# Inverting triangles as 64x64 diagonal blocks in a two-layer hybrid decoder kernel on one core

## What is computed

```python
def step(S, inp):
    r_t, w_t, k_t, v_t, kk_t, a_t = inp
    sa = jnp.einsum('bhvk,bhk->bhv', S, -kk_t)
    S = S * w_t[:, :, None, :] + sa[..., None] * (kk_t * a_t)[:, :, None, :] + v_t[..., None] * k_t[:, :, None, :]
    return S, jnp.einsum('bhvk,bhk->bhv', S, r_t)
```

## Time and profile before

| what | value |
|---|---|
| median of 3 runs | 1758.09 us (1756.2 to 1758.63) |
| the profiled execution's own time | 1759.65 us |
| its span, first to last instruction | 1757.8 us |
| TensorE busy | 97% |
| VectorE (DVE) busy | 74% |
| ScalarE (ACT) busy | 58% |
| chain that ended last | PE 86%, DVE 6%, ACT 4%, issue 2%, DMA 1% |
| granted TensorE clock, mean | 0.988 of full speed |

### The profile page before, as it was taken

The page is one execution under the profiler, slowest core; times in us unless marked ns, Lnnn a source line. Parts: engine busy times, 40 slices in busy tenths (PEclk is TensorE's granted clock), DMA queues, the critical chain, the costliest instruction groups (busy, mean ns, idle before and its releaser), DMA issues.

```text
span 1757.8 us, 27919 instructions
## 1 busy us (share of the span) xinstructions
PE 1700.0 (97%) x10846; PEld 1516.8 (86%) x10846; DVE 1294.9 (74%) x1185; ACT 1027.5 (58%) x995; POOL 0.9 (0%) x8
## 2 busy tenths in 40 slices
PE   7999999999999899999999999999999999999997
PEld 7999888889999899988888888888888888888885
DVE  5856665475445675757646889888898989898987
ACT  5563454454344456445444677767777777777775
POOL 0000000000000000000000000000000000000000
PEclk9999999999999999999999999999999999999999
DMA  8433331456565443333145889999998999999993
GB/s 287 144 98 108 109 120 61 166 164 196 175 191 185 136 159 116 101 120 121 49 145 197 322 329 392 343 362 375 337 393 319 375 332 392 335 364 355 363 387 137
DMA packets 252072, 411.25 MB, mean 234 GB/s; under 512 B 8400, under 2 KB 133712, under 8 KB 251344
## 3 DMA queue, kind: packets, MB, share of 16 engines
q1 hardware_dynamic: 249728, 401.20, 64.8%
q10 hardware_dynamic: 2256, 8.82, 1.3%
HBM read 407.89 MB, written 2.10 MB: 233 GB/s over the span
## 4 chain that ended last, share of the span: by engine, by line
PE 86%; DVE 6%; ACT 4%; issue 2%; DMA 1%; SPq 0%; DVEq 0%; ACTq 0%
PE W L459 18%; PE W L461 18%; PE W L460 18%; PE Y L459 6%; PE Y L460 6%; PE Y L461 6%; PE Y L681 2%; PE Y L675 2%; PE W L568 1%; ACT w_hi L1116 1%; PE Y L568 1%; PE Y L650 1%; DMA raw<-w_in 1%; DVE xt L1744 1%; PE Y L912 1%
## 5 line engine op out<-in xcount | busy, mean ns | idle before, releaser
L1585 DVE TENSOR_TENSOR w_lo<-raw,w_hi 128x2048 fp32r<-128x2048 f32 x114 | 261.2, 2292 | 197.4 <-ACT w_hi L1116 196.3
L459 PE MATMUL W<-w_lo,x_hi 128*128 128x512 f32 (+1 forms) x1120 | 390.3, 349 | 1.3 <-DVE x_lo L1883 1.1
L461 PE MATMUL W<-w_hi,x_hi 128*128 128x512 f32 (+1 forms) x1120 | 386.0, 345 | 0.0
L460 PE MATMUL W<-w_hi,x_lo 128*128 128x512 f32 (+1 forms) x1120 | 385.6, 344 | 0.0
L1592 DVE TENSOR_TENSOR w_lo<-raw,w_hi 128x2048 fp32r<-128x2048 f32 x144 | 329.7, 2289 | 45.1 <-ACT w_hi L1122 45.0
L1122 ACT ACTIVATE w_hi<-raw 128x2048 fp32r<-128x2048 f32 x144 | 276.1, 1917 | 73.1 <-PE Y L461 40.0
L459 PE MATMUL W<-x_lo,w_hi 128*128 128x256 f32 x992 | 292.9, 295 | 10.2 <-DVE w_lo L2104 8.9
L1592 DVE TENSOR_TENSOR w_lo<-raw_more,w_hi 128x2048 fp32r<-128x2048 f32 x120 | 275.0, 2292 | 28.5 <-ACT w_hi L1122 28.3
L460 PE MATMUL W<-x_hi,w_lo 128*128 128x256 f32 x992 | 282.8, 285 | 0.0
L461 PE MATMUL W<-x_hi,w_hi 128*128 128x256 f32 x992 | 282.5, 285 | 0.0
L1122 ACT ACTIVATE w_hi<-raw_more 128x2048 fp32r<-128x2048 f32 x120 | 230.5, 1921 | 64.0 <-PE W L461 41.1
(11 more groups left out here) (306 smaller groups left out, 2025.0 us busy)
## 6 DMA issues: line engine op xcount, KB each, us to landing
raw<-w_in SPq DMA_DIRECT2D x124, 512.0 KB, 4.6
raw<-moe_gate SPq DMA_DIRECT2D x48, 1024.0 KB, 6.1
raw<-moe_up SPq DMA_DIRECT2D x48, 1024.0 KB, 6.7
raw<-moe_down SPq DMA_DIRECT2D x48, 1024.0 KB, 5.0
raw_more<-moe_gate SPq DMA_DIRECT2D x40, 1024.0 KB, 7.2
raw_more<-moe_up SPq DMA_DIRECT2D x40, 1024.0 KB, 6.7
raw_more<-moe_down SPq DMA_DIRECT2D x40, 1024.0 KB, 6.0
raw<-w_branch SPq DMA_DIRECT2D x24, 512.0 KB, 4.6
```

The source lines that it names most:

```text
L459: nc.tensor.matmul(out_ap, lhs[0], rhs[1], start=start, stop=False)
L460: nc.tensor.matmul(out_ap, lhs[1], rhs[0], start=False, stop=False)
L461: return nc.tensor.matmul(out_ap, lhs[0], rhs[0], start=False, stop=stop)
L1585: V.tensor_tensor(w_lo[u % 3][:], raw[u % 3][:], w_hi[u % 3][:].bitcast(F32), ALU.subtract)\
```

## The change

- **Form.** The inverse of a 128x128 triangle is put together from its two diagonal blocks of 64x64. `ac` holds those blocks of A, for each u the upper one in partitions 0 to 63 and the lower one in 64 to 127; `compact` (ScalarE, two copies per pass) fills it. `xt`, `xn` (X), `mc` (masked A, and later the product) have 64 columns per u.
- **Levels 1 to 5** work on both blocks: per u two products of 64x64 by 64x64 (`blocks`), one on rows 0 to 63 into partitions 0 to 63, one on rows 64 to 127 into 64 to 127 of the same bank. Copies, additions and masks have half the columns.
- **The turned form** is no longer a transposition but such a product with the identity, in two halves.
- **Level 6** (`TOP`) computes the off-diagonal block: per u one product of 64x64 from the full `sc` with output in partitions 64 to 127, a copy of 64 rows by ScalarE, one product back into partitions 0 to 63, and a copy by DVE into a second column block of `xt`. ScalarE copies the lower diagonal block beside it.
- **`cu`** has two products per head: 64 rows and 64 weight columns for the first half of the output, 128 rows and 64 weight columns for the second.
- **Order.** `compact` stands after the second `scores` entry of each pass; in pass 0 conv 2 is split into front and back, and `masks` stands between them. On DVE the split of weights in the front of conv 2 therefore comes ahead of the masks.
- **Memory and constants.** `dsh` and `td` move under `pr`; `fin1` and `fin2` lie in `mc` and `xn`. The masks are loaded in compact form: the constants come in 6 transfers in place of 1.

```diff
...
-C_COS = C_LEV + LEVELS * P
+C_COS = C_LEV
+D_COS = C_LEV + LEVELS * P
+TOP = LEVELS - 1
...
-    ("front", "conv", 1), ("scores", 0, 0), ("back", "conv", 1), ("scores", 0, 1),
-    ("masks", 0), ("units", "conv", 2, 3), ("invert", 0), ("shift", 3),
+    ("front", "conv", 1), ("scores", 0, 0), ("back", "conv", 1), ("scores", 0, 1), ("compact", 0),
+    ("front", "conv", 2), ("masks", 0), ("back", "conv", 2), ("invert", 0), ("shift", 3),
...
-    ("front", "qkv", 4), ("scores", 1, 1), ("back", "qkv", 4), ("rope", 1),
+    ("front", "qkv", 4), ("scores", 1, 1), ("compact", 1), ("back", "qkv", 4), ("rope", 1),
...
-        dsh = sb("dsh", [P, 2, T])
+        cm = sb("cm", [P, LEVELS, HD])
...
-        t1, t2, t3, t4, t6, td = (sb(f"t_{n}", [P, 2, T]) for n in ("a", "r", "k", "g", "b", "d"))
+        t1, t2, t3, t4, t6 = (sb(f"t_{n}", [P, 2, T]) for n in ("a", "r", "k", "g", "b"))
...
-        xm = sb("xm", [P, 8, P])
-        xt = sb("xt", [P, 8, P])
-        mt = sb("mt", [P, 8, P])
+        xt = sb("xt", [P, 8, 2, HD])
+        xn, mc = (sb(name, [P, 8, HD]) for name in ("xn", "mc"))
+        dsh = sb("dsh", [P, 2, T])
+        td = sb("t_d", [P, 2, T])
+        ac = sb("ac", [P, 8, HD])
...
         def tiles(ap, n=2):
...
-        def level_mask(v):
-            return cst[:, C_LEV + v * P:C_LEV + (v + 1) * P].unsqueeze(1).to_broadcast([P, 4, P])
...
-        fin1, fin2 = (xm[:, 4 * i:4 * i + 4, :].rearrange("p (m c) t -> p m (c t)", c=2) for i in range(2))
+        def each_of_4(column):
+            return cm[:, column, :].unsqueeze(1).to_broadcast([P, 4, HD])
...
+        fin1, fin2 = (a[:].rearrange("p (m c) t -> p m (c t)", c=4) for a in (mc, xn))
...
+            def load_constants():
+                sp.dma_start(cst[:, 0:C_LEV], const[:, 0:C_LEV]).then_inc(sem("cst_full"), 16)
+                for half in HALVES:
+                    masks = const[half, C_LEV:C_LEV + TOP * P].rearrange("p (v c) -> p v c", c=P)[:, :, half]
+                    sp.dma_start(cm[half, 0:TOP, :], masks).then_inc(sem("cst_full"), 16)
+                    sp.dma_start(cm[half, TOP, :], const[half, C_ID + half.start:C_ID + half.stop]).then_inc(sem("cst_full"), 16)
+                sp.dma_start(cst[:, C_COS:C_END], const[:, D_COS:D_COS + 2 * T]).then_inc(sem("cst_full"), 16)
...
-                                sp.dma_start(cst[:], const).then_inc(sem("cst_full"), 16)
+                                load_constants()
...
             def lora_w(l, p):
...
-                    pe.wait_ge(sem("cst_full"), 16)
+                    pe.wait_ge(sem("cst_full"), 96)
...
+            def blocks(c, bank, left, right):
...
+                for u in range(4):
+                    for half in HALVES:
+                        last = nc.tensor.matmul(tiles(bank[:, 0:4 * HD], 4)[half, u, :], left[half, 4 * c + u, :],
+                                                right[half, 4 * c + u, :], start=True, stop=True)
+                return last
...
             def untranspose(n, v):
...
-                    for h in range(4):
-                        last = transpose(tiles(Y[c][:], 4)[:, h, :], xt[:, 4 * c + h, :])
+                    for u in range(4):
+                        for half in HALVES:
+                            last = nc.tensor.matmul(tiles(Y[c][:, 0:4 * HD], 4)[half, u, :], xt[half, 4 * c + u, 0, :],
+                                                    ident[half, half], start=True, stop=True)
...
             def level(l, p, v):
...
-                at = 2 * (LEVELS - 1) * n + 2 * (v - 1)
+                at = 2 * TOP * n + 2 * (v - 1)
...
-                    pe.wait_ge(sem("mt_ready"), at + c + 1)
-                    for h in range(4):
-                        last = nc.tensor.matmul(tiles(Y[c][:], 4)[:, h, :], mt[:, 4 * c + h, :], xm[:, 4 * c + h, :],
-                                                start=True, stop=True)
+                    if v < TOP:
+                        pe.wait_ge(sem("mc_ready"), 2 * (TOP - 1) * n + 2 * (v - 1) + c + 1)
+                        last = blocks(c, Y[c], mc, xn)
+                    else:
+                        for u in range(4 * c, 4 * c + 4):
+                            last = nc.tensor.matmul(tiles(Y[c][:, 0:4 * HD], 4)[HD:P, u % 4, :], sc[0:HD, u, 0, HD:P], xn[0:HD, u, :],
+                                                    start=True, stop=True)
...
-                    for h in range(4):
-                        last = nc.tensor.matmul(tiles(Y[2 + c][:], 4)[:, h, :], mt[:, 4 * c + h, :], xt[:, 4 * c + h, :],
-                                                start=True, stop=True)
+                    if v < TOP:
+                        last = blocks(c, Y[2 + c], mc, xt[:, :, 0, :])
+                    else:
+                        for u in range(4 * c, 4 * c + 4):
+                            last = nc.tensor.matmul(tiles(Y[2 + c][:, 0:4 * HD], 4)[0:HD, u % 4, :], mc[HD:P, u, :], xt[HD:P, u, 0, :],
+                                                    start=True, stop=True)
...
-                if v < LEVELS - 1:
+                if v < TOP:
...
+                if c == 0:
+                    pe.wait_ge(sem("column_ready"), n + 1)
...
-                    last = nc.tensor.matmul(Y[1][:, hc], xt[:, 4 * c + h, :], g_s[:, h, :], start=True, stop=True)
+                    nc.tensor.matmul(Y[1][0:HD, hc], xt[0:HD, 4 * c + h, 0, :], g_s[0:HD, h, :], start=True, stop=True)
+                    last = nc.tensor.matmul(Y[1][HD:P, hc], xt[:, 4 * c + h, 1, :], g_s[:, h, :], start=True, stop=True)
...
+            def compact(l, p):
+                n = 2 * l + p
+                act.wait_ge(sem("score_ready"), 8 * n + 8)
+                for half in HALVES:
+                    last = A(ac[half], sc[half, :, 0, half], ACT.Copy)
+                last.then_inc(sem("ac_ready"), 1)
...
             def copy_x(n, v):
-                at = 2 * (LEVELS - 1) * n + 2 * v
+                at = 2 * TOP * n + 2 * v
...
-                    A(xm[:, 4 * c:4 * c + 4, :], tiles(Y[c][:], 4), ACT.Copy).then_inc(sem("x_ready"), 1)
+                    A(xn[:, 4 * c:4 * c + 4, :], tiles(Y[c][:, 0:4 * HD], 4), ACT.Copy).then_inc(sem("x_ready"), 1)
...
             def invert(l, p):
...
             def level(l, p, v):
...
-                at = 2 * (LEVELS - 1) * n + 2 * (v - 1)
+                at = 2 * TOP * n + 2 * (v - 1)
+                rows = slice(0 if v < TOP else HD, P)
...
-                    A(mt[:, 4 * c:4 * c + 4, :], tiles(Y[c][:], 4), ACT.Copy).then_inc(sem("mx_ready"), 1)
-                if v < LEVELS - 1:
+                    A(mc[rows, 4 * c:4 * c + 4, :], tiles(Y[c][:, 0:4 * HD], 4)[rows], ACT.Copy).then_inc(sem("mx_ready"), 1)
+                if v < TOP:
...
+                else:
+                    act.wait_ge(sem("xt_ready"), 2 * LEVELS * n + 2 * TOP)
+                    A(xt[HD:P, :, 1, :], xt[HD:P, :, 0, :], ACT.Copy).then_inc(sem("column_ready"), 1)
...
-            def mask_level(n, v, c):
...
-                return V.tensor_tensor(mt[:, 4 * c:4 * c + 4, :], sc[:, 4 * c:4 * c + 4, 0, :], level_mask(v), ALU.mult)
+            def mask_level(v, c):
...
+                return V.tensor_tensor(mc[:, 4 * c:4 * c + 4, :], ac[:, 4 * c:4 * c + 4, :], each_of_4(v), ALU.mult)
...
             def masks(l, p):
...
+                dve.wait_ge(sem("ac_ready"), n + 1)
...
-                    link(mask_level(n, 0, c))
-                    mark(V.tensor_tensor(xt[:, 4 * c:4 * c + 4, :], mt[:, 4 * c:4 * c + 4, :],
-                                         ident.unsqueeze(1).to_broadcast([P, 4, P]), ALU.add),
+                    link(mask_level(0, c))
+                    mark(V.tensor_tensor(xt[:, 4 * c:4 * c + 4, 0, :], mc[:, 4 * c:4 * c + 4, :], each_of_4(TOP), ALU.add),
...
-                    mark(mask_level(n, 1, c), "mt_ready", 2 * (LEVELS - 1) * n + c + 1)
+                    mark(mask_level(1, c), "mc_ready", 2 * (TOP - 1) * n + c + 1)
...
             def level(l, p, v):
...
-                    dve.wait_ge(sem("dxt_done"), 2 * (LEVELS - 1) * n + 2 * (v - 1) + c + 1)
-                    mark(V.tensor_tensor(xt[:, 4 * c:4 * c + 4, :], xt[:, 4 * c:4 * c + 4, :], tiles(Y[2 + c][:], 4), ALU.add),
-                         "xt_ready", 2 * LEVELS * n + 2 * v + c + 1)
-                if v < LEVELS - 1:
+                    dve.wait_ge(sem("dxt_done"), 2 * TOP * n + 2 * (v - 1) + c + 1)
+                    dx = tiles(Y[2 + c][:, 0:4 * HD], 4)
+                    if v < TOP:
+                        step = V.tensor_tensor(xt[:, 4 * c:4 * c + 4, 0, :], xt[:, 4 * c:4 * c + 4, 0, :], dx, ALU.add)
+                    else:
+                        step = V.tensor_copy(xt[0:HD, 4 * c:4 * c + 4, 1, :], dx[0:HD])
+                    mark(step, "xt_ready", 2 * LEVELS * n + 2 * v + c + 1)
+                if v < TOP - 1:
...
-                        mark(mask_level(n, v + 1, c), "mt_ready", 2 * (LEVELS - 1) * n + 2 * v + c + 1)
```

(3 more changed lines are left out.)

## The result

The changed kernel takes **1743.99 us** (median of 4 runs, 1742.24 to 1744.49) against 1758.36 for the kernel before (median of 4 runs beside it, 1756.2 to 1759.26). The ratio is 0.9918, 95% interval [0.9901, 0.9935]: faster by 14.4 us, where 16 were forecast.

A forecast was written before the change was run, and what follows sets the result against it. It took TensorE's queue, busy 97% of the span, as the bound. Per layer -4.6 (pass 0) - 9.4 (pass 1) + 5.8 (cu) + 0.3 (rope) = -7.9, two layers -16: 1742 us against 1758.1, range 1728 to 1769.

The forecast's parts named there:

- The bound: Whole kernel: TensorE, busy 97% of the span, sets the end; a microsecond off its working queue comes off the end.
- The pair price: Inversion products: two 64x64 tiles on different halves overlap, 0.058 us a pair, 0.46 per group of four heads.
- Rival 1: Inversion products: halves sharing a PSUM bank don't overlap, 0.109 a pair, +10 us per layer, 1778 us; chance 0.15.
- The levels: Inversion, per layer: levels 1, 2, 4 and 5 of pass 0 save 5.8 us; pass 1's three stretches save 9.4.
- Level 6: Pass 0's last inversion level: -1.4 us per layer, with ScalarE's copies still behind a w_hi copy.
- The first turned form: Pass 0, after conv 2: TensorE waits for masks behind VectorE's weight split, 3.8 us instead of 0.8, +3.0 per layer.
- cu: Eight in the kernel: alternating tile shapes drain the array, 0.26 us a product, 2.26 each, +5.8 us per layer.
- rival 2: cu does not drain and levels come closer to 0.053 us a pair: 1732 us; chance 0.17.
- Rope: Pass 1's last rope: compact delays ScalarE by 1.1 us, of which about 0.3 arrives, +0.3 per layer.
- Constants: Kernel start: six transfers instead of one end at 20.7 us; nothing charged, upper end +3.
- Rival 3: Gain eaten by cu at its upper end (+9), late constants (+3) and late DVE orders (+5): 1759 us; chance 0.08.

The follow-up runs named there:

- e2: Changed kernel with cu issued as one full 128x128 tile per head, its empty slot zeroed by ScalarE: 1730.16 us.
- e8: Changed kernel with every group of turned-form products issued twice into the same bank: 1763.24 us, single run.
- e4: Changed kernel with the upper half's products issued before the lower half's in levels 1 to 5, not alternating: 1758.8 us, single run.
- e1: Changed kernel with the first turned form's masks placed before the front of conv 2: 1737.68 us.
- e3: Changed kernel with cu's four 64-row products issued first and its four 128-row products after them: 1736.74 us.
- e6: Changed kernel with pass 1's compact copy moved from before rope to before gate1: 1752.5 us.
- e7: Changed kernel with masks before conv 2's front, full tile in cu, exponentials behind level 3 and pass 1's compact before gate1: 1724.22 us.
- e9: As e7, but pass 1's compact copy stands behind the second transposing of the probabilities: 1720.67 us.
- e11: As e9, but without the move of the exponentials behind level 3: 1722.95 us.
- e10: Changed kernel with only masks before the front of conv 2 and the full tile in cu: 1724.01 us.

## Why the prediction was right, and where it was off

- **The bound.** TensorE's own queue sets the end, and a stretch's time comes off the span: shown by the table, whose sum of -16.8 stands against a span 15.7 shorter, and by e2 and e8, which took 10.8 off and put 21.0 on in the stretches and moved the span by -13.6 and +19.1, the clock's share apart.
- **The pair price.** Forecast 0.058 a pair and 0.46 a group; measured 0.059 and 0.46. Rival 1 falls: both halves write one bank, in other partitions, and run side by side. The Trainium skill's rule (TensorEngine Tiling (Array Packing), Gotcha 1: PSUM Pressure), that different row tiles can't access one bank at the same time, does not hold in this form here (starts 0.03 apart); the measurement decides. What the overlap is worth is seen in e4, where losing a part of it in levels 1 to 5 cost 10.2 us in the levels, 14.8 with the clock.
- **The levels.** -5.9 against -5.8, and -9.5 against -9.4 in pass 1. Within pass 1 the three stretches were -3.6, -2.7 and -3.2 against -3.5, -2.7 and -3.15.
- **Level 6 was mis-sized:** -1.4 forecast, -2.1 measured in each layer. I had it wait for ScalarE's copies behind w_hi as before. The timeline after shows products at 144.52 and 145.68 and the next projection at 146.75, with the copies between them at 145.25 and no wait for w_hi: ScalarE's w_hi ends at 144.3 there, ahead of the level. That is read from the trace; no run tried it.
- **The first turned form,** +3.0 forecast, +3.3 and +3.7 measured. The chain was as written down, ending 0.3 earlier than forecast; conv 2's projections ended 0.6 earlier too (the kernel's first records do), so the gap is longer by the difference. Why layer 1's is 0.45 more was not traced. e1 shows that it was the order in the list: the stretch falls from 4.06 to 1.17. The 0.37 by which that is still above 0.80 is near the 0.34 that the prediction reckoned for changing the tile and back.
- **cu,** +5.8 forecast, +5.3 measured (2.14 us each instead of 2.26). The prediction's terms 0.05 + 0.05 + 0.05 + 0.10 make 0.25, and it wrote 0.26; measured 0.255. Of the 1.33 us that a cu grew by, e3 shows 0.84 to be the changes from product to product, and e2 that the full tile gives back all of it; rival 2 falls by that. What rival 2 had for it, that the two shapes share the column half, is not so in the code: one product writes partitions 0 to 63 of the bank, the other 64 to 127, from different columns of `xt`.
- **Rope,** +0.3 forecast, +0.7 measured: ScalarE's copies of the scores take 1.27 us, not 1.1, and more of it reached rope's last product. e6, e7, e9 and e11 show the cause: with the copy elsewhere, 0.62.
- **Constants,** nothing forecast and nothing seen: the six transfers end by 18.0, not 20.7, the next load is issued at 18.11 (17.83 before), and no product waits. No run undid them; that they cost nothing is read from the trace alone.
- **Rival 3** had its terms too high in each place.
- **What the sum left out** is the clock. It took 1.3 us back of a gain that was forecast as 16; the prediction took durations from rows at full clock and never asked what longer gaps on TensorE do to the records behind them.
- **How much was luck.** The mechanism was right part by part, but the sum is closer than its parts: per layer, level 6 and cu together came out 1.2 better than forecast, the first turned form and rope 0.7 to 1.1 worse. The stretches so made 16.8 where 15.8 was forecast, and the clock, left out, took 1.3 of that.

## What to carry to other kernels

Here, products on two halves of the array ran side by side when they alternated in the queue, also into one bank, in other partitions of it. A product whose shape alternated with its neighbour's paid 0.14 us for each change, so group by shape, or pad to the full tile where that is 0.2 us a product (two records of 0.1). When an operation is moved in a hand-written order, write down for every engine what it was doing before and what now stands ahead of it: the exponentials' move and compact's first only moved a wait, while the masks' used time in which VectorE had stood idle. To price a part, double it: what the time grows by is what the part costs on the path.

## What the runs showed of the hardware that was not expected

- Gaps on TensorE can cost more than themselves. After 3 to 4 us in which it was busy for 0.6 to 1.8, the granted clock fell to the 1.2 GHz level for 3 us (0.52 in the changed kernel at 84 to 87 us) or for 6.6 us (0.51 in e1 at 113 to 119.6), and it cost 1.5 us of projections in the first case, 1.7 of projections and 1.4 of level 3 in the second. Experiment 3, and level 3 in the changed kernel, show that not every such gap is followed by a fall. From the projection units of a kernel the clock took from 3.0 us (e10) to 13.2 us (e6), so that kernels whose stretches differ by 2 us can't be ranked by their time alone.
- Each half of the array keeps its own pace of one 64x64 record per 0.058 us (two of these make a product in this type), and does so also while the other half works. When the queue holds one half's products first (e4), the other half starts 0.29 us late, after five records, and not after all eight.
- The change between a 64x64 and a 128x64 tile, both on the upper rows, costs as well: 0.15 us from the last record of one shape to the first of the next (e3), where records of one shape follow by 0.058, and so 0.26 from product to product, two records each, when each is another shape (the changed kernel).
